# Residue-class passes for the two dilated head groups of a prompt attention, and a new order of its passes

## The reference, cut to what matters

```python
idx = q_idx[:, None] - dil * jnp.arange(n_keys)[None, :]
ok = idx >= 0
...
s = jnp.where(ok[None, :, None, :], s, -jnp.inf)
...
o_a = moba_attend(qb[:, :, :N_MOBA_HEADS], pb, kb, vb, kmean)
for g, (win, dil) in enumerate(SWA_GROUPS):
    o_g, l_g = dilated_attend(...)
wgt = jax.nn.softmax(jnp.stack(lses), axis=0)
o_b = jnp.einsum('gbqh,gbqhd->bqhd', wgt, jnp.stack(outs).astype(jnp.float32))
```

## Time and profile before

| | us |
|---|---|
| median of 3 runs | 1552.17 (1552.16 to 1554.07) |
| profiled execution, its own time | 1551.67 |
| its span in the profile | 1549.5 |
| TensorE, VectorE, ScalarE busy | 1474.2, 909.3, 562.4 |
| granted TensorE clock, mean | 0.984 |

### The profile page before, as it was taken

One profiled execution on the slowest core, in us unless ns is written; L12 is line 12 of the kernel. 1 busy time (PEld: TensorE's weight loads), 2 busy tenths in 40 slices (PEclk: granted clock), 3 DMA queues, 4 the chain that ended last, 5 costly groups with the idle time before them and its releaser, 6 DMA issues.

```text
span 1549.5 us, 24277 instructions
## 1 busy us (share of the span) xinstructions
PE 1474.2 (95%) x9372; PEld 1307.5 (84%) x9372; DVE 909.3 (59%) x1734; ACT 562.4 (36%) x1062; POOL 60.4 (4%) x90
## 2 busy tenths in 40 slices
PE   7999898899999999999999999989999999999995
PEld 6888666689999999878798888768999999998784
DVE  4644354386666666635641877765866666664536
ACT  3222277333333333422324433541433333343231
POOL 1012200010000000000100100110100000000000
PEclk9999999999999999999999999989999999999998
DMA  5235323633222222534322211362123222214211
GB/s 200 85 102 178 109 70 111 178 84 93 82 80 81 81 80 73 196 138 157 133 62 77 82 55 55 117 207 56 55 82 81 81 81 81 81 54 133 85 66 61
DMA packets 153912, 153.56 MB, mean 99 GB/s; under 512 B 12375, under 2 KB 123223, under 8 KB 153383
## 3 DMA queue, kind: packets, MB, share of 16 engines
q1 hardware_dynamic: 149938, 139.54, 29.6%
q0 software_dynamic: 3904, 13.07, 2.4%
HBM read 140.76 MB, written 21.91 MB: 105 GB/s over the span
## 4 chain that ended last, share of the span: by engine, by line
PE 86%; DVE 7%; ACT 3%; issue 2%; DMA 1%; POOL 1%; SPq 0%; ACTq 0%; DVEq 0%; POOLq 0%
PE ps L704 70%; PE ps L715 5%; PE ps L685 3%; PE ps L1075 1%; PE ps L779 1%; PE ps L813 1%; ACT w_hi L1215 1%; DVE x_reg L1806 1%; ACT attn_side L1201 1%; DVE w_lo L1593 1%; PE ps L996 1%; POOL w_lo L2196 1%; DVE x_reg L1788 1%; DVE ln_stats L1795 1%; DVE x_reg L1810 1%
## 5 line engine op out<-in xcount | busy, mean ns | idle before, releaser
L704 PE MATMUL ps<-xh_reg,w_hi 128*128 128x288 f32 x1552 | 463.6, 299 | 6.5 <-POOL w_lo L2196 3.5
L704 PE MATMUL ps<-xh_reg,w_lo 128*128 128x288 f32 x1552 | 459.3, 296 | 0.0
L704 PE MATMUL ps<-xl_reg,w_hi 128*128 128x288 f32 x1552 | 459.2, 296 | 0.0
L704 PE MATMUL ps<-w_hi,xh_reg 128*128 128x512 f32 x768 | 307.9, 401 | 7.9 <-DVE xl_reg L1847 3.4
L704 PE MATMUL ps<-w_hi,xl_reg 128*128 128x512 f32 x768 | 301.7, 393 | 0.0
L704 PE MATMUL ps<-w_lo,xh_reg 128*128 128x512 f32 x768 | 301.4, 392 | 0.0
L704 PEld LDWEIGHTS ps<-xh_reg,w_hi 128*128 128x128 f32 x1552 | 293.5, 189 | 8.7 <-issue 6.2
L704 PEld LDWEIGHTS ps<-xl_reg,w_hi 128*128 128x128 f32 x1552 | 293.6, 189 | 0.0
L704 PEld LDWEIGHTS ps<-xh_reg,w_lo 128*128 128x128 f32 x1552 | 293.4, 189 | 0.0
L1593 DVE TENSOR_TENSOR w_lo<-raw,w_hi 128x2048 fp32r<-128x2048 f32 (+1 forms) x51 | 111.4, 2184 | 241.8 <-ACT w_hi L1215 241.8
L704 PEld LDWEIGHTS ps<-w_hi,xh_reg 128*128 128x128 f32 x768 | 145.8, 190 | 40.0 <-issue 7.2
(11 more groups left out here) (207 smaller groups left out, 1459.7 us busy)
## 6 DMA issues: line engine op xcount, KB each, us to landing
raw<-in_ffn_w_up SPq DMA_DIRECT2D x88, 512.0 KB, 4.9
raw<-in_ffn_w_down SPq DMA_DIRECT2D x40, 512.0 KB, 4.6
raw<-in_attn_w_in SPq DMA_DIRECT2D x24, 512.0 KB, 4.8
raw<-in_gla_w_in SPq DMA_DIRECT2D x24, 512.0 KB, 4.5
out_swa_s<-in_state_swa_kv SPq DMA_DIRECT2D x16, 496.0 KB, 6.4
x_reg<-in_x_prompt SPq DMA_DIRECT2D x8, 512.0 KB, 8.3
raw<-in_gla_w_out SPq DMA_DIRECT2D x8, 512.0 KB, 4.6
out_swa_p<-arena POOLq DMA_DIRECT2D x18, 128.0 KB, 3.0
```

What stands on the lines that cost most here:

```text
L704: mm = pe.matmul(out, lhs(i, a), rhs(i, b), start=first and i == 0 and a + b == 0, stop=last and i == ks - 1 and a == 1)
```

## The change

The rows of the prompt are dealt to four classes by their position modulo 4. In the projection, the keys and queries of groups 2 and 3 are written to `qkT` class by class, and for units 10 and 11 the activations are read with a step of four columns, so that the values come out class by class. Groups 2 and 3 then need only the keys of the own class: eight class passes (four classes, two pairs) with two blocks of 128 by 128 for each head, unscaled outputs kept in `o_class`, and their greatest scores and sums turned back to the order of the tiles. Eight tile passes follow with groups 0 and 1 alone (6, 5, 4 and 2 blocks for each head in tiles 3, 2, 1 and 0), in the order tile 3, 0, 3, 0, 2, 1, 2, 1; each brings the class part to its own greatest score, merges it, and spreads three scales over the head's columns by small products. The first scores of pass `p + 2` stand between the turning of pass `p` and its values. The diff, cut:

```diff
+CLASS_UNITS = [UNIT_NO[("attn_in", c_)] for c_ in (10, 11)]
...
+        PASSES = [("class", r, pair) for pair in range(2) for r in range(PQ)]
+        PASSES += [("tile", qi, pair) for qi, pair in ((3, 0), (0, 0), (3, 1), (0, 1), (2, 0), (1, 0), (2, 1), (1, 1))]
+        CLASSES = 2 * PQ
...
-            sp.wait_ge(scale_done, 4)
+            sp.wait_ge(valued, 11)
             load_values(4)
-            sp.wait_ge(scale_done, 6)
+            sp.wait_ge(valued, 16)
             load_values(5)
...
+                if n in CLASS_UNITS:
+                    three_products(ps[:, t, :], lambda i, a: parts[a][:, k0 + i, 0:NP].rearrange("p (j r) -> p r j", r=PQ)[:, t, :],
+                                   lambda i, b: w[b][:, i, :], kn, first, last).then_inc(steps, 1)
...
+            def turn_scales(p):
+                q = p - CLASSES
+                pe.wait_ge(inverse_ready, q + 1)
+                turn([(0, rden[:, q % 4, :])])
+
+            def spread_scales(p):
+                pe.wait_ge(turned_out, batch_of("scales", p) + 1)
...
+                for k in range(3):
+                    mm = pe.matmul(ps[:, bank, k * P:(k + 1) * P], spread_of[:, k, :], scale_rows, start=True, stop=True)
+                mm.then_inc(turned, batch.one())
...
+            scores_of(0, 0)
+            scores_of(1, 1)
+            for p in range(len(PASSES)):
+                turn_probs(p, 0)
+                if p and not is_class(p - 1):
+                    spread_scales(p - 1)
+                if p + 1 < len(PASSES):
+                    for e in events(p + 1)[1:]:
+                        scores_of(p + 1, e)
+                if not is_class(p):
+                    turn_probs(p, 1)
+                if p + 2 < len(PASSES):
+                    scores_of(p + 2, events(p + 2)[0])
+                values(p)
+                if not is_class(p):
+                    turn_scales(p)
+                if p in TO_ROWS:
+                    stats_to_rows(TO_ROWS[p])
+                if p in TO_COLS:
+                    stats_to_cols(TO_COLS[p])
+            spread_scales(len(PASSES) - 1)
...
+                if kind == "class":
+                    act.activation(buf[:, 0:2 * P], buf[:, 0:2 * P], ACT.Exp, bias=class_nm[:, p, b:b + 1], scale=ATT_SCALE,
+                                   accum_out=class_stat[:, p, 2 + b:3 + b]).then_inc(probs, 1)
+                    return
+                q = (p - CLASSES) % 4
+                act.activation(class_exp[:, q, b:b + 1], tile_stat[:, pair, at, b:b + 1], ACT.Exp, bias=nm[:, q, 2 + b:3 + b],
+                               scale=ATT_SCALE)
...
+            for p in range(len(PASSES)):
+                take_probs(p, 0)
+                if p and not is_class(p - 1):
+                    take_spread(p - 1)
+                if not is_class(p):
+                    take_probs(p, 1)
+                if p + 1 < len(PASSES):
+                    exps(p + 1, 0)
+                    exps(p + 1, 1)
+                if is_class(p):
+                    take_class_out(p)
+                else:
+                    if not is_class(p - 1):
+                        round_out(p - 1)
+                    take(scale_rows, lambda bank: bank[0:6, 0:P])
...
+            def last_scores(p):
...
+                take_scores(p, events(p)[1])
+                dve.wait_ge(s_read, 2 * events(p)[1] + 2)
+                dve.wait_ge(turned_out, batch_of("cols", pair) + 1)
+                dve.tensor_tensor(mx[:, q, 2:4], mx[:, q, 2:4], tile_stat[:, pair, at, 0:2], ALU.max).then_inc(vec, vs.one())
                 settle()
+                dve.tensor_scalar(nm[:, q, :], mx[:, q, :], -ATT_SCALE, None, ALU.mult).then_inc(nm_ready, 1)
...
+            for p in range(len(PASSES)):
+                if not is_class(p):
+                    invert(p)
+                if p + 1 < len(PASSES):
+                    last_scores(p + 1)
+                if p and not is_class(p - 1):
+                    scale_out(p - 1)
+                if p + 2 < len(PASSES):
+                    first_scores(p + 2)
+                if p and not is_class(p - 1):
+                    rest_of_out(p - 1)
```

More of the change, by code:

```diff
@@ L756, in _ @@
                         turn_rope(r)
[L759 to L776, removed]
-                    for b in range(2):
[L778 to L781, removed]
@@ L797, in values, with pair_buffer, scores_of @@
-            def values(n):
-                qi, pair = query_tile(n), n % 2
-                blocks = prob_blocks(qi)
-                bank = (4, 7)[n % 2]
-                if n >= 2:
-                    pe.wait_ge(o_made, n - 1)
+            def pair_buffer(p):
+                return pair_scores[(p + 1) % 2]
+            def scores_of(p, e):
+                kind, at, pair = PASSES[p]
+                if e == 0:
+                    pe.wait_ge(turned_out, UP0)
+                    pe.wait_ge(qk_read, 4 * NTILE)
+                    pe.wait_ge(v_read, 2 * NTILE)
+                if e >= 2:
+                    pe.wait_ge(s_read, 2 * (e - 1))
+                q0, q1 = at * P, (at + 1) * P
+                if kind == "class":
+                    for g in (2, 3):
+                        for b in range(2):
+                            rows, c = slice(HD * b, HD * b + HD), 2 * g + pair
+                            mm = pe.matmul(ps[:, 2 * (e % 2) + b, (g - 2) * P:(g - 1) * P], qkT[rows, c, q0:q1],
+                                           qkT[rows, 8 + c, q0:q1], start=True, stop=True)
+                else:
+                    g = e % 2
+                    k0 = max(0, at - 1) * P if g else 0
+                    for b in range(2):
+                        rows, c = slice(HD * b, HD * b + HD), 2 * g + pair
+                        mm = pe.matmul(ps[:, 2 * (e % 2) + b, 0:q1 - k0], qkT[rows, c, q0:q1],
+                                       qkT[rows, 8 + c, k0:q1], start=True, stop=True)
+                mm.then_inc(s_ready, 1)
@@ L803, in values @@
+            def values(p):
+                _, _, pair = PASSES[p]
+                blocks = prob_blocks(p)
+                bank = (4, 7)[p % 2]
+                if p >= 2 and is_class(p - 2):
+                    pe.wait_ge(o_classed, p - 1)
+                elif p >= 2:
+                    pe.wait_ge(o_made, p - 2 - CLASSES + 1)
                 seen = 0
                 for merged in range(2):
-                    mine = [i for i, blk in enumerate(blocks) if (blk[2] > 0) == bool(merged)]
+                    mine = [i for i, blk in enumerate(blocks) if is_class(p) and merged == 0 or not is_class(p) and blk[2] == merged]
@@ L1684, in first_scores @@
+            def first_scores(p):
+                if p >= 2:
+                    dve.wait_ge(turned, probs_turned(p - 2))
+                elif p == 1:
                     dve.wait_ge(turned, UP0)
```

335 lines of the change are left out of this document (186 added, 149 removed).

## The result

The changed kernel is slower: median 1563.34 us (1559.33 to 1565.61, four runs) beside 1552.16 us of the kernel before (1548.86 to 1554.07, four runs). The ratio is 1.0072, 95% interval 1.0055 to 1.0089. Forecast was 1552.9, and the range ended at 1562.0.

The account below looks back on a forecast made before the run. TensorE bound the kernel, with ScalarE close behind and setting the new stage's pace: 3.05 + 16.7 + 4.1 + 46.6 = 70.4 us against 70.4, plus 0.75 behind it, giving 1552.9 us; range 1546 to 1562.

Parts of the forecast that it names:

- The start: Prompt attention, from the first scores to the first turning of a class pass: 3.05 us, against 8.0 before.
- the class loop: Eight class passes: each turning follows the last by 2.38 us, through take and exponentials; seven steps make 16.7 us.
- ScalarE busy 51 or more: Sign of being right: ScalarE's busy time in the prompt's attention stage, in us, against 49.7 before.
- the second rival: Projection, units 10 and 11: weight loads with a step of four set the products' step; 1557 to 1567 us, chance 0.20.
- The late load of values: Rival behind the stage: 3 us of issuing value loads falls wholly on keys TensorE waits for; 1556 us, chance 0.07.
- the first rival: Tile passes: ScalarE's waits get covered, half of 11 us of waiting goes; 1547.4 us, chance 0.24.
- class turnings over 2.8 us apart: Sign of being wrong, in the class passes, where turnings were forecast 2.4 us apart.
- TensorE's clock falls: Rival in the attention stage: TensorE's waits in every pass lower its clock; 4 to 10 us, 1557 to 1563, chance 0.05.
- TensorE's part: Sum of TensorE's work in the prompt's attention stage: falls by about 16 us, from 61.3 to some 45.
- TensorE busy under 48 us: Sign of being right: TensorE's busy time in the attention stage, with idle time put down to ScalarE.
- Sum 46.6: Eight tile passes: loops through scale rows, spread, second scores and exponentials, 4.6 to 6.5 us each, total 46.6 us.
- 16.7 + 4.1: Attention stage: seven class-pass steps, 16.7 us, plus the step to the first tile pass, 4.1 us.

Follow-up runs that it names:

- fills_light: The changed kernel plus 22 idle TensorE products, whose result nobody reads, placed in its waits; median 1557.84 us, ratio 1.0052 to the kernel before.
- plain_loads: The changed kernel with activations of units 10 and 11 read without a step, values of groups 2 and 3 in wrong order; 1566.69 us, ratio 1.0080.
- fill_all: The changed kernel plus 100 idle TensorE products, at the start, in class and tile passes and before the samples' keys; 1588.26 us, ratio 1.0228.

## Why the prediction was wrong

**What held.** The start (3.03 us for 3.05) and the class loop at full clock (2.38 for 2.38). ScalarE busy 51 or more: 54.6, though the sum had 51. Idle time of TensorE put down to ScalarE. The strided loads at almost nothing: 0.8 us, where the second rival had 4 to 14. The late load of values: waits of 3.6 us here and 3.9 to 5.4 in the other kernels with the change, beside 4.85. ScalarE's waits got no cover, so the first rival fell. A sign of being wrong came too: class turnings over 2.8 us apart (3.25 and 2.90), where the clock was at half.

**First step that failed: the weight on the clock.** The forecast ran every loop at full clock and gave the rival "TensorE's clock falls" a chance of 0.05. Its place and price were right: "4 to 10 us, 1557 to 1563", measured 8.1 us of the stage and 1563.3, though the total reached the rival's upper end only because the loops were longer too (below); the pairs of tile passes lost 1.6, 1.3, 0.7 and 3.0 us (13.7, 13.3, 13.1, 16.4 beside 12.1, 12.0, 12.4, 13.4), and the class passes at half clock 0.87 and 0.52. What failed was the argument against it, "through the stage before, with waits of its own, the clock stayed at its full level". That stage had TensorE busy for 61.3 of 70.4 us; my own sum put the new one at some 45 of the same 70. I compared the length of single waits, which stayed short (none above 1.9 us), and not the whole of them: TensorE was idle for 9.1 of 70.4 us before, and for 15.2 of 82.1 now. The stage before was no evidence for one that my own sum made so much idler: the rows at hand said only that the clock holds in a busy stage and falls behind a wait of 4.8 us, and what lies between the two was open.

The Trainium skill (TensorE: Matmul & The Clock Gate, A second HAM failure mode: psum-queue depth-cycling) describes a kernel in which frequent small idle times of TensorE between groups of products made the clock swing between its two levels. The trace agrees: five falls in 90 us, none behind a wait above 1.9 us. The Trainium skill (TensorE: Matmul & The Clock Gate, Terms) puts the penalty at the throttled time times one half; by that estimate the 34 us more at half level (41 after, 6.8 before, from 180 to 295 us) would cost 17. Measured is less, 8.1 in the stage and 1.3 behind it: in a stretch at half clock TensorE waits less (from 225 to 230 us not at all), so a part of the slower work goes into waits that were there anyway.

**TensorE's part.** That sum was mis-sized as well. "TensorE busy under 48 us" did not come: it was busy for 66.9 us in the change, part of it at half clock, and for 65.3 in fills_light at full clock. Without the 9.5 of the idle products that leaves some 56, where the sum had 45 and the stage before 61.3: about 5.5 us of busy time went, not 16. One term can be read above: three spreading products take 0.86 us (255.67 to 256.53), 0.29 each, where the sum had the 0.13 of a transposition, so 24 of them cost 3.8 us more. The rest I have not taken apart. It was not this that made the kernel slower, but TensorE had less to give away than the sum said.

**Second step: the tile loops.** "Sum 46.6" measured 49.8 with the clock held (207.25 to 257.07), 0.4 of it the last idle product; "16.7 + 4.1" measured 21.2. Most steps stand within 0.5 us of the forecast: 0 to 3, 4.7 for 4.6; 0 to 2, 5.1 for 5.1; 1 to 2, 5.7 for 5.8; 3 to 0 the second time, 6.8 for 6.3. Two were too small: the first tile to the second, 7.4 for 6.5, since ScalarE's take of the class sums (4 by 512, written with a step of four) takes 1.09 us and stands ahead of the take of the first probabilities; and the last tile, 6.8 with that idle product for 5.7. These terms have no experiment of their own; they are read from fills_light's timeline.

So the 14.0 us of the profiled executions are 8.1 for the clock in the stage, 3.6 for loops longer than laid out, 1.0 ahead of the stage, and 1.3 behind it, where the clock stays at half until 273.6 us (in fills_light, at full clock there until 277, the samples' part takes 46.9). The sum of the forecast for the same four was 0, 0, 0 and 0.75. These sizes are those of single executions: with the 79.3 us of plain_loads, whose attention is the same, the clock in the stage would have 5.3, and the 1.0 ahead of the stage is no more than first scores differ between profiles.

**A check over runs.** 45 runs of the kernel before, beside the experiments, list a span and a mean clock each. At 0.987 the span was 1543.2 us, at 0.984 the median 1548.0 (20 runs), at 0.981 1552.3 (15 runs): about 1.4 us for each 0.001. The four runs of the change have 0.978 and 1557.2 us, three times 0.973 and 1561.4, 1561.5 and 1563.5. Carried on with the same slope, the kernel before would take 1556.5 and 1563.5. The change's runs lie on the line of the kernel before within 2.1 us. The line doesn't part the clock from the loops, since a fall costs less where TensorE waits anyway; it shows that a slower run of either kernel is mostly one with a lower mean clock.

**What stays open.** How much less work for TensorE, or which pattern of waits, lets the clock fall, was not measured; idle products show only that filling the waits holds it. That the new order at full clock would be as fast as the old is not shown: the best such profile, 73.4 us of stage, is 3 us above the old one's 70.4.

## What to carry to other kernels

Work taken from TensorE is won only if the loop through the other engines gets shorter too. If it doesn't, the work turns into waiting, and the clock column of the stage is to be read before anything else: many waits under 2 us in a row brought 38 us at half clock here, one wait of 4.85 us in the kernel before 6.8. Where a forecast makes an engine idler, the clock of the stage before is no evidence for the stage after. A few products into an unused bank, shorter than the wait that they stand in, tell a clock effect from a longer loop, and can be worth keeping; a dose longer than the wait goes onto the path (fill_all).

## What the runs showed of the hardware that I had not expected

- The clock fell to half behind waits of 1.9 us and less, five times in one stage, and stayed there for 20 us at the end, while TensorE was shown busy for 13.2 of 15 us: a busy share read at half clock says little.
- A load of weights with a step of 16 bytes takes about 0.31 us instead of 0.19, but moves the product's step only from 0.227 to 0.235.
- Eight products, 3.7 us in all, into a bank nobody reads, make the kernel before about 2.5 us faster (0.3 to 4.5).
- Between runs of one kernel the mean clock varies from 0.981 to 0.988, and the span follows it by about 1.4 us for each 0.001.
